# Two turnovers between blocks done per half of the tokens, and the pool branch placed among the last attention heads

## What is computed

```python
# block one
h = rms_norm(x, g_norm) * (1.0 + scl) + shift            # mod = c @ w_ada + b_ada
u_pool, z_pool, q, k, v, z_attn, m_pool, m_attn = split(h @ w_in)
y_pool = (multiscale_pool(u_pool, w_pool_grp, pool_scale) * silu(z_pool)) @ w_pool_up
y_attn = (moba_attention(rope(q), rope(k), v) * silu(z_attn)) @ w_attn_up
x = x + gate * ((sigmoid(m_pool) * y_pool + sigmoid(m_attn) * y_attn) @ w_out)
x = rms_norm(x, g_final)
# block two
h = rms_norm(x, g_norm_mix) * (1.0 + sc1) + sh1
mix = concat(retention(h), nsa(h)) @ w_out_2
x = x + ga1 * mix
h = rms_norm(x, g_norm_ffn) * (1.0 + sc2) + sh2
x = x + ga2 * peer(h)
out = rms_norm(x, g_final_2)
```

## Time and profile before

| | us |
|---|---|
| median of 3 runs | 1352.95 (1351.39 to 1353.01) |
| the profiled execution, its own time | 1350.58 |
| span of that execution | 1348.8 |

### The profile page before, as it was taken

One profiled execution on the slowest core, in us unless ns is written; L12 is line 12 of the kernel. 1 busy time (PEld: TensorE's weight loads), 2 busy tenths in 40 slices (PEclk: granted clock), 3 DMA queues, 4 the chain that ended last, 5 costly groups with the idle time before them and its releaser, 6 DMA issues.

```text
span 1348.8 us, 17892 instructions
## 1 busy us (share of the span) xinstructions
PE 1271.4 (94%) x6818; PEld 996.1 (74%) x6818; DVE 838.2 (62%) x1815; ACT 516.3 (38%) x979; POOL 317.7 (24%) x150
## 2 busy tenths in 40 slices
PE   4999999959999797999999999999999999999996
PEld 2444546425555557999999999999988888888885
DVE  5545542245442635289994899999856666666656
ACT  2011111001122313354445666555554544545453
POOL 0000000000000000078887777776710000000000
PEclk9899998979899897999999999999999999999998
DMA  9966662324441112245554445544456665666564
GB/s 380 395 276 275 257 257 109 126 84 190 184 187 63 63 63 110 78 155 177 185 188 157 158 157 161 162 156 148 155 174 229 221 225 188 226 190 192 196 189 154
DMA packets 54516, 244.20 MB, mean 181 GB/s; under 512 B 6944, under 2 KB 7328, under 8 KB 42016
## 3 DMA queue, kind: packets, MB, share of 16 engines
q1 hardware_dynamic: 54000, 242.34, 51.2%
q10 hardware_dynamic: 432, 0.72, 0.2%
HBM read 240.94 MB, written 2.10 MB: 180 GB/s over the span
## 4 chain that ended last, share of the span: by engine, by line
PE 90%; DVE 5%; DMA 1%; issue 1%; ACT 1%; SPq 1%; POOL 0%; POOLq 0%; DVEq 0%
PE banks L868 12%; PE bank L868 11%; PE bank L1194 9%; PE bank L1190 9%; PE bank L1191 9%; PE banks L1230 4%; PE bank L1236 4%; PE banks L1233 4%; PE bank L1230 4%; PE banks L1236 4%; PE bank L1233 4%; PE banks L1204 3%; DMA G<-in_ada 1%; PE banks L1061 1%; DVE tab L1314 1%
## 5 line engine op out<-in xcount | busy, mean ns | idle before, releaser
L605 POOL TENSOR_TENSOR split_r<-ring,split_r 128x1024 fp32r<-128x1024 f32 x128 | 307.9, 2406 | 163.2 <-ACT split_r L788 163.1
L788 ACT ACTIVATE split_r<-ring 128x1024 fp32r<-128x1024 f32 x256 | 269.4, 1053 | 181.9 <-PE bank L1194 181.9
L1190 PE MATMUL bank<-h_high_r,split_r 128*128 128x256 f32 x1024 | 252.1, 284 | 1.7 <-ACT split_r L788 1.7
L1191 PE MATMUL bank<-h_low_r,split_r 128*128 128x256 f32 x1024 | 251.9, 284 | 0.0
L1190 PEld LDWEIGHTS bank<-h_high_r,split_r 128*128 128x128 f32 x1024 | 197.0, 192 | 1.9 <-issue 1.9
L1733 DVE TENSOR_TENSOR split_r<-ring,split_r 128x1024 fp32r<-128x1024 f32 x128 | 156.8, 1225 | 65.6 <-ACT split_r L788 65.6
L1191 PEld LDWEIGHTS bank<-h_low_r,split_r 128*128 128x128 f32 x1024 | 197.1, 192 | 0.0
L868 PE MATMUL banks<-G 128*128 128x512 f32 x320 | 141.8, 599 | 2.4 <-issue 2.4
L1194 PE MATMUL bank<-h_high_r,split_r 128*128 128x256 f32 x1024 | 143.7, 283 | 0.2 <-POOL split_r L605 0.2
L1194 PEld LDWEIGHTS bank<-h_high_r,split_r 128*128 128x128 f32 x1024 | 132.1, 192 | 0.5 <-POOL split_r L605 0.5
L868 PE MATMUL bank<-G 128*128 128x512 f32 (+1 forms) x288 | 126.0, 594 | 3.6 <-DVE G L1432 3.6
(11 more groups left out here) (332 smaller groups left out, 1764.6 us busy)
## 6 DMA issues: line engine op xcount, KB each, us to landing
ring<-in_down SPq DMA_DIRECT2D x128, 512.0 KB, 3.5
ring<-in_up SPq DMA_DIRECT2D x128, 512.0 KB, 3.6
G<-in_ada SPq DMA_DIRECT2D x32, 1024.0 KB, 11.3
G<-in_in SPq DMA_DIRECT2D x32, 1024.0 KB, 7.2
G<-in_out SPq DMA_DIRECT2D x8, 1024.0 KB, 8.2
G<-in_wq SPq DMA_DIRECT2D x8, 1024.0 KB, 6.0
tab<-in_ada SPq DMA_DIRECT2D x4, 1024.0 KB, 6.5
G<-in_poolup SPq DMA_DIRECT2D x2, 1024.0 KB, 6.1
```

What stands on the lines that cost most here:

```text
L605: pool.tensor_tensor(wsplit[:, j % SPLIT, 1, :], raw[:, j % RAW, :], wsplit[:, j % SPLIT, 0, :].bitcast(F32), ALU.subtract).then_inc(low_r ...
L788: nc.scalar.activation(wsplit[:, n % SPLIT, 0, :], raw[:, n % RAW, :], ACT.Copy).then_inc(high_ready, 1)
L1190: mm(o, w[0][:, c, :], h_high[:, c, :], start=(c == 0), stop=False)
L1191: mm(o, w[0][:, c, :], h_low[:, c, :], start=False, stop=False)
```

## The change

Four things are done.

1. The pool branch moves into the heads of block one: poolT before the last panel in1 9 (head 6), pool under head 7, upT and the first two banks of poolup in the round after. The gating of the attention output gets a step of its own, "y", after the heads. The load of the modulation panel ada2 7 moves behind poolup and attnup in `STREAM`, and VectorE sums it at the first attnup bank.
2. Both turnovers are done per tile by `turn_over`: variance and norm of tile 0 stand before the last "wout" of tile 1, and the transposes of tile 0 right behind it. In block one the first half of the projection in2 5 stands between the transposes of tile 0 and those of tile 1, and a projection waits only for its own tile.
3. The sums of squares move from VectorE to ScalarE, one for each half tile, as each is added (`Square` with an accumulated output). In block one VectorE makes `xg = x * gfin` beside x, and ScalarE squares both.
4. One power serves both norms of block one: with v the variance of x plus eps, and m the mean square of x*gfin, GpSimd raises v and `eps*v + m` to -1/2 in one instruction; the first scales xg to the new x, the second scales xg directly to the normed input of block two.

The diff, cut to its core:

```diff
@@ STREAM
-             (("in1", 8), ("ada2", 6)), (("in1", 9), ("ada2", 7))):
+             (("in1", 8), ("ada2", 6))):
     STREAM += [(*a, PANEL, "pe"), (*b, PANEL, "dve")]
-STREAM += [("poolup", None, PANEL, "pe"), ("attnup", None, PANEL, "pe"), ("out1", 0, PANEL, "pe"), ("out1", 1, PANEL, "pe")]
+STREAM += [("in1", 9, PANEL, "pe"), ("poolup", None, PANEL, "pe"), ("attnup", None, PANEL, "pe"), ("ada2", 7, PANEL, "dve"),
+           ("out1", 0, PANEL, "pe"), ("out1", 1, PANEL, "pe")]
...
+BLOCK_ONE = sum(n < AT["out1", 0] for n in ADA)
@@ steps()
+    def turn_over(b, between):
+
+        out.extend([("wout", b, 0, 0), ("wout", b, 0, 1), ("wout", b, 1, 0), ("var", b, 0), ("norm", b, 0), ("wout", b, 1, 1),
+                    ("xT", b + 1, 0, 0), ("var", b, 1), ("xT", b + 1, 0, 1), ("norm", b, 1)])
+        out.extend(between)
+        out.extend(("xT", b + 1, 1, half) for half in range(2))
...
-    heads(0, [[("panel", *p)] for p in IN1_LATER])
+    later = [[("panel", *p)] for p in IN1_LATER]
+    later[6] = [("poolT", 0), ("poolT", 1)] + later[6]
+    later += [[("pool", 0), ("pool", 1)], [("upT", 0), ("upT", 1), ("up", "poolup", 0, 0), ("up", "poolup", 0, 1)]]
+    heads(0, later)
+    out.append(("y",))
     for n in ada_after(AT[("poolup", None)], ada):
         out.append(("ada", n))
-    out.extend(("poolT", half) for half in range(2))
-    out.extend(("pool", t) for t in range(NT))
+    out.extend(("up", "poolup", 1, half) for half in range(2))
     out.extend(("oT", t) for t in range(NT))
-    out.extend(("upT", t) for t in range(NT))
-    out.extend(("up", "poolup", t, half) for t in range(NT) for half in range(2))
     out.extend(("up", "attnup", t, half) for t in range(NT) for half in range(2))
+    for n in ada_after(AT[("out1", 0)], ada):
+        out.append(("ada", n))
     out.extend(("mT", 0, t, half) for t in range(NT) for half in range(2))
-    out.extend(("wout", 0, half, t) for half in range(2) for t in range(NT))
-    out.extend(("xT", 1, t, half) for t in range(NT) for half in range(2))
-    panel("in2", 5)
+    turn_over(0, [("proj", "in2", 5, 0)])
+    for item in [("proj", "in2", 5, 1)] + [("ada", n) for n in ada_after(AT[("in2", 5)], ada)]:
+        out.append(item)
...
-    out.extend(("wout", 1, half, t) for half in range(2) for t in range(NT))
-    out.extend(("xT", 2, t, half) for t in range(NT) for half in range(2))
+    turn_over(1, [])
@@ GpSimd
+            pool.wait_ge(var_ready, 1)
+            pool.tensor_tensor(rstd, ss, half_neg[:, 0:2], ALU.pow).then_inc(rstd_ready, 1)
+            for t in range(NT):
+                pool.wait_ge(var_ready, 2 + t)
+                pool.tensor_tensor(r_pair[:, t], v_pair[:, t], half_neg[:, 0:2], ALU.pow).then_inc(rstd_ready, 1)
@@ ScalarE
-                        if half == 0:
-                            high_part(0, 1)
-                elif s == ("xT", 2, 0, 0):
-                    high_part(0, 0)
+                elif kind == "xT" and s[1] == 2:
+                    high_part(0, s[3])
...
-                if s == ("wout", 0, 1, 1):
-                    act.wait_ge(x_ready, 1)
+                if kind == "wout":
+                    _, b, half, t = s
+                    k, c = 4 * b + 2 * half + t, slice(half * 512, (half + 1) * 512)
+                    act.wait_ge(x_added, k + 1)
+                    ins = nc.scalar.activation(xn[1][:, t, c], xv[:, t, c], ACT.Square, accum_out=sqx[:, t, half:half + 1])
+                    if b == 0:
+                        act.wait_ge(xg_ready, k + 1)
+                        ins = nc.scalar.activation(xg_squares[:, t, c], xg[:, t, c], ACT.Square, accum_out=sqg[:, t, half:half + 1])
+                    ins.then_inc(squares_b, 1)
+                if s == ("norm", 0, 1):
+                    act.wait_ge(x_ready, NT)
                     act.dma_start(gateA, d["gate2"].partition_broadcast(P)).then_inc(gateA_in, 16)
@@ TensorE
-                    if name in ("in1", "in2") and t == 0 and (name, i) in (("in1", 2), ("in2", 5)):
-                        for tt in range(NT):
-                            for half in range(2):
-                                evacuated(pe_, ("xT", b, tt, half))
+                    if (name, i) in (("in1", 2), ("in2", 5)):
+                        for half in range(2):
+                            evacuated(pe_, ("xT", b, t, half))
...
-                        pe_.wait_ge(h_high_ready, 2 + 2 * half)
+                        pe_.wait_ge(h_high_ready, 3 + half)
@@ VectorE
+            def mean_square(dst, sums, t, eps):
+
+                link(ts(dst, sums[:, t, 0:1], sums[:, t, 1:2], 1.0 / D, ALU.add, ALU.mult))
+                if eps:
+                    link(ts(dst, dst, eps, None, ALU.add))
+
+            def block_variance(b, t):
+
+                dve.wait_ge(squares_b, 4 * b + 3 + t)
+                if b == 0:
+                    mean_square(v_pair[:, t, 0:1], sqx, t, EPS)
+                    mean_square(v_pair[:, t, 1:2], sqg, t, None)
+                    stt(out=v_pair[:, t, 1:2], in0=v_pair[:, t, 0:1], scalar=EPS, in1=v_pair[:, t, 1:2], op0=ALU.mult, op1=ALU.add)\
+                        .then_inc(var_ready, 1)
...
+            def normed(b, t):
+
+                dve.wait_ge(rstd_ready, 2 + 2 * b + t)
+                if b == 0:
+                    ts(xn[1][:, t, :], xg[:, t, :], r_pair[:, t, 1:2], None, ALU.mult).then_inc(xn_ready, 1)
+                    ts(xv[:, t, :], xg[:, t, :], r_pair[:, t, 0:1], None, ALU.mult).then_inc(x_ready, 1)
...
+                    if s == ("up", "attnup", 0, 0):
+                        while accs[0] < BLOCK_ONE:
+                            next_acc()
...
+                    ins = tt(xv[:, t, c], xv[:, t, c], sc, ALU.add)
+                    ins.then_inc(x_added, 1)
+                    dve.wait_ge(x_added, 4 * b + 2 * half + t + 1)
+                    if b == 0:
+                        tt(xg[:, t, c], xv[:, t, c], gfin[:, c], ALU.mult).then_inc(xg_ready, 1)
+                    elif half == 0:
+                        query_low(t)
+                elif kind == "var":
+                    block_variance(*s[1:])
+                elif kind == "norm":
+                    normed(*s[1:])
```

More of the change, by code:

```diff
@@ L179 @@
 for s in STEPS:
-    if s[0] in ("pv", "cmpO", "retO"):
+    if s[0] in ("pv", "cmpO", "retO", "var", "norm", "y"):
         continue
@@ L371, in program @@
         sq = col(4)
+        sqx, sqg = col(NT, 2), col(NT, 2)
+        v_pair, r_pair = col(NT, 2), col(NT, 2)
+        xg = tmp(11264, NT, D)
+        xg_squares = tmp(13312, NT, D)
         assert s_at[0] <= 694, s_at[0]
@@ L587, in _ @@
             pool.tensor_scalar(ss, ss, 1.0 / D, EPS, ALU.mult, ALU.add).then_inc(var_ready, 1)
-            for k in range(3):
-                pool.wait_ge(var_ready, k + 1)
-                pool.tensor_tensor(rstd, ss, half_neg[:, 0:2], ALU.pow).then_inc(rstd_ready, 1)
+            pool.wait_ge(var_ready, 1)
[3 more added lines that the diff above has]
+                pool.tensor_tensor(r_pair[:, t], v_pair[:, t], half_neg[:, 0:2], ALU.pow).then_inc(rstd_ready, 1)
             evacuated(pool, ("proj", "in2", 5, 0))
@@ L600, in _ @@
             pool.tensor_tensor(rr, cs, half_neg, ALU.pow).then_inc(gn_rstd, 1)
-            pool.wait_ge(var_ready, 4)
-            pool.tensor_tensor(rstd, ss, half_neg[:, 0:2], ALU.pow).then_inc(rstd_ready, 1)
+            for t in range(NT):
+                pool.wait_ge(var_ready, 4 + t)
+                pool.tensor_tensor(rstd[:, t:t + 1], ss[:, t:t + 1], half_neg[:, 0:1], ALU.pow).then_inc(rstd_ready, 1)
             for j in range(P):
@@ L607, in _ @@
             for t in range(NT):
-                pool.wait_ge(var_ready, 5 + t)
+                pool.wait_ge(var_ready, 6 + t)
                 pool.tensor_tensor(rstd[:, t:t + 1], ss[:, t:t + 1], half_neg[:, 0:1], ALU.pow).then_inc(rstd_ready, 1)
@@ L1528, in _ @@
                     dve.sem_inc(ret_p, 1)
-                elif kind == "poolT" and s[1] == 0:
+                elif kind == "y":
                     evacuated(dve, ("proj", "in1", 9, 1))
@@ L1559, in _ @@
                     c = slice(half * 512, (half + 1) * 512)
-                    sc = tmp(9216, 512)
+                    sc = tmp(15872, 512)
                     bank_free(stt(out=sc, in0=src[:, :], scalar=0.5 if b == 0 else 1.0, in1=gateA[:, c], op0=ALU.mult, op1=ALU.mult), s)
                     evacuated(dve, s)
-                    link(tt(xv[:, t, c], xv[:, t, c], sc, ALU.add))
-                    if b == 1 and (half, t) in ((0, 1), (1, 0)):
-                        query_low(half)
-                    if half == 1 and t == 1:
-                        if b == 0:
-                            row_sums(xv, xn[1])
-                            for q in range(NT):
-                                link(stt(out=xv[:, q, :], in0=xv[:, q, :], scalar=rstd[:, q:q + 1], in1=gfin,
-                                         op0=ALU.mult, op1=ALU.mult))
```

(10 more changed lines are left out.)

30 lines of the change are left out of this document (14 added, 16 removed).

## The result

The changed kernel takes 1337.89 us (median of four runs, 1336.64 to 1341.55). The kernel before took 1352.74 beside it (four runs, 1351.39 to 1353.01). The ratio is 0.9897, 95% interval 0.9875 to 0.9918: 1% faster, 14.9 us. The forecast was 1338.6. The profiled execution took 1336.64 with a span of 1334.8; before it was 1350.58 with 1348.8, so the two traces differ by 14.0 us.

A forecast was written before the change was run, and what follows sets the result against it. TensorE, with 90% of the chain, was taken as the bound, so only its waits and low clock could give time. Gains of 5.2 + 6.9 + 2.3 = 14.4 us from 1352.95 gave 1338.6, range 1334.3 to 1346.

The forecast's parts named there:

- The tail: Last head's score to block one's first output matmul: waits and half clock of 9.6 us shrink, gaining 5.2 (3.4 to 6.4).
- The waits: TensorE's remaining tail waits: 0.3 for the softmax, 1.6 and 1.0 for pool's products, 0.2 for the copy behind oT.
- The cover of ada2 7: VectorE's 6.0 us modulation sum, moved under attnup, costs nothing; up to 1 us with that cover gone.
- rival (d): Slower, for instance because out1 1's load waits behind poolup's last use in SyncE's queue; 1357 if landing takes 50; chance 0.03.
- Turnover one: Block one's output end to the end of projection in2 5: 26.6 instead of 33.5 us, gaining 6.9 (5.1 to 8.6).
- the margin: In turnover one, t=0's 6.05 us norm chain fits under the last output bank's 6.87, with 0.8 us to spare.
- Turnover two: Block two's output end to the first query matmul: 8.8 us instead of 11.1, gaining 2.3 (0.9 to 3.0).
- The squares and the table: ScalarE's squares need no table load, so none priced; by the skill's estimate one would cost 1.9 us in turnover one.
- The median: Whole kernel: the runs' median lies 2.4 us above the profiled execution, giving 1338.6 where the profiled one gives 1336.2.
- (a): Short waits keep the clock low in the tail and both projection halves, 3.0 us each place; 1344 to 1346; chance 0.14.
- (b): The norm chain of t=0 misses its cover under the last output bank, turnovers gain little; about 1347 us; chance 0.09.
- (c): The clock survives the waits of the tail and between the projection halves; gain over 18, 1334 us; chance 0.08.

The follow-up runs named there:

- turn_only: The changed kernel with the pool branch, its panels and ada2 7 put back where they were, both turnovers by halves; 1342.85 us, ratio 0.9932 to before.
- earlier: The changed kernel with poolT and pool one head earlier, upT still behind the last score; 1337.37 us, ratio 0.9904 to before.
- the fills: Two runs of the changed kernel with unread matmuls in three waits: 13, 12 and 4 took 1337.83 us; 7, 6 and 2 took 1332.27 us.
- after: The changed kernel itself, as first measured and traced; 1337.89 us, ratio 0.9897 to the kernel before.
- after_again: The changed kernel run once more, unedited, as anchor for the follow-up runs; 1339.76 us, ratio 0.9915 to before.
- earlier_fill: The changed kernel with the pool branch one head earlier and 7, 6 and 2 unread matmuls in three waits; 1330.12 us, ratio 0.9843 to before.

## Why the prediction was right

**The tail: 5.2 foretold, 4.95 found.** The waits were foretold at 0.3, 1.6, 1.0 and 0.2, 3.2 with rounding; they are 0.23, 1.32, 0.36 and 0.25, 2.2. The clock was foretold at 1.2; it costs 2.7 from the last score to the output (204.00 to 245.19 is 41.2 us, less 36.3 of the same pieces at full clock, less the 2.2). 0.9 of it is in the up banks (28.4 for 27.5), 1.2 in the two banks of upT, which took 2.4 us with their wait and would have taken 0.9. The two errors belong together: the second wait is short because the transposes ahead of it were slow. One sum, two terms wrong in opposite ways.

**The cover of ada2 7.** VectorE did its sum from 232.20 to 238.2, and the four evacuations followed until 244.0; TensorE's mT waits for none of them. The cost was nothing, as foretold. out1 1's load, rival (d), shows no wait either.

**Turnover one: 6.9 foretold, 7.39 found.** From the output to the first projection 6.1 was foretold and 5.58 found; between the halves 3.85 and 3.48. The clock: 1.7 foretold for the first half and 3.07 found (9.94 less 6.87), 1.2 and 0.24 for the second. All lie within the ends given, but for 3.07, just beyond its upper end of 3.0. At the same waits `turn_only` had 1.93 and 1.93, and `earlier` 1.93 and 0.24, so rows of before could tell neither the split between the halves nor their sum to better than some 1.7 us (3.3, 3.9 and 2.2 in all); that the 2.9 foretold came within 0.4 of the 3.3 is in part luck. The transposes of t=0 come without a wait; the margin is 1.5 and not 0.8, since the steps and hand-overs are each a little shorter than costed: the chain takes 5.4 us, from 265.84 to 271.2, and not 6.05.

**Turnover two: 2.3 foretold, 2.45 found**: the query matmul starts 8.61 behind the output (8.8 foretold), and the slow groups behind it are unchanged, 6.6 us where before had 6.8.

**The squares and the table.** No load came; the square shares a table with what runs around it. The estimate by the Trainium skill (ScalarE: Activation LUTs, Table sets), 1.9 us back, is not borne out: the list of fillers that it rests on doesn't name the square, and the trace shows no load before it.

**The median.** 1350.58 - 14.4 was 1336.2 for the profiled execution, which took 1336.64. The rest, from 14.8 at the three places to 14.0 of span, is scatter at the start of the kernel, from X to Y and in the last phase; the other runs show it with no edit there. The forecast put the median 2.4 above the profiled execution and it lies 1.25 above, so a part of the closeness of 1338.6 to 1337.89 is luck, too.

**The rivals.** (a) had the right mechanism and too high a price for each place: the fills show some 2.8 us in the first turnover and 3 at the queries, but the second of these the kernel before paid too, so a change of the turnover neither wins nor loses it. (b) and (d) did not come; (c) neither: the clock held nearly untouched (0.24) across the gap between the halves, and nowhere else. What the prediction didn't see is that the order it costed in turnover one is itself longer there than the plain one, by 3.3 us (2.3 with the clock held): it took 3.85 for the gap between the halves, from the right rows, and never asked what that gap would be if the projection weren't split.

## What to carry to other kernels

Cost each wait of TensorE with what stands behind it: in after's turnovers and the query groups behind them, idle matmuls of the right length in the waits gave back 5.8 us of clock. Twice as many of them overshot the waits, and the time was 1.9 us under after_again instead of 7.5. When a piece of work is put between two transposes to fill a wait, write down the wait that then opens behind it; ScalarE's drain is hidden only if it lies under the work and not between its parts. And look at a moved step's copy in its own queue: `earlier` gained nothing until the copy of upT was queued ahead of the exponentials.

## What the runs showed of the hardware

An fp32 matmul is two records for TensorE, and 384 columns take 0.64 us at full clock (0.32 a record), 512 columns 0.86 (13.73 for sixteen matmuls, 32 records). I had planned for half.

The granted clock behind the same wait is not a constant: 9.94 and 7.11 us for the two halves in after (twice, to 0.05), 8.80 and 8.80 in `turn_only`, 8.80 and 7.10 in `earlier`, and with the wait filled 7.10 and 7.10. The first up bank behind one wait took 5.40 in `earlier` and 3.70 in `earlier_fill`. The two traces of one program, after and after_again, agree; traces of programs whose code at that place is the same differ. Whether it goes by the program or by the execution isn't shown, since every other program has one trace, and the times of one program can lie 6.7 us apart (`earlier`). The Trainium skill (TensorE: Matmul & The Clock Gate, "What's actually happening") says that the point where the clock changes varies with where the first matmuls happen to fall. The traces don't contradict it, but none of them shows its cause; what they show is that 1.1 to 1.7 us of one bank or half move with it.
